# First layer of a hybrid diffusion backbone on one core: where the modulation chunks run

## What is computed

```python
for l in range(DEPTH):                                   # DEPTH = 2
    sh1, sc1, g1, sh2, sc2, g2 = split(silu(c) @ w_ada[l] + b_ada[l], 6)   # modulation, one row per stream
    hm = modulate(rmsnorm(x, norm_pre_mix[l]), sh1, sc1)
    rq, rk, rv, rg, nq, nk, nv = split(hm @ w_in[l])
    y_ret = retention_output(retention_bidir(rq, rk, rv), rg)              # 4 heads
    y_na = neighbourhood_attention(nq, nk, nv, cached keys and values)     # 8 heads of 64
    g_ret, g_na = split(sigmoid(hm @ w_gate[l]), 2)
    x = x + g1 * rmsnorm((g_ret * (y_ret @ w_ret_out[l]) + g_na * (y_na @ w_na_out[l])) @ w_o[l])
    hf = modulate(rmsnorm(x), sh2, sc2)
    x = x + g2 * rmsnorm((silu(hf @ w_ffn_gate[l]) * (hf @ w_ffn_up[l])) @ w_ffn_down[l])
```

## Time and profile before

| | us |
|---|---|
| median of 3 runs | 2136.46 |
| lowest and highest run | 2135.92, 2137.36 |
| profiled execution: span from its first to its last instruction | 2134.6 |
| median less that span (what lies around the span; the profiled execution's own time is not noted apart from it) | 1.9 |

### The profile page before, as it was taken

The page is one execution under the profiler, slowest core; times in us unless marked ns, Lnnn a source line. Parts: engine busy times, 40 slices in busy tenths (PEclk is TensorE's granted clock), DMA queues, the critical chain, the costliest instruction groups (busy, mean ns, idle before and its releaser), DMA issues.

```text
span 2134.6 us, 34256 instructions
## 1 busy us (share of the span) xinstructions
PE 2103.7 (99%) x14114; PEld 2011.7 (94%) x14114; DVE 1545.8 (72%) x2477; ACT 931.8 (44%) x1494; POOL 101.6 (5%) x195
## 2 busy tenths in 40 slices
PE   7999999999999999999999999999999999999998
PEld 6999999999989999999889999999999899999997
DVE  5688767477757887887877886755864668787786
ACT  5655432476334433332476554225753544233332
POOL 0000010110000000000000000001100000000000
PEclk9999999999999999999999999999999999999999
DMA  7333354233334222222433333532233322222223
GB/s 301 114 118 128 104 172 144 99 101 133 134 115 162 70 81 98 80 79 80 168 131 101 117 119 134 166 126 80 85 119 129 129 60 80 79 80 81 98 79 138
DMA packets 63099, 246.08 MB, mean 115 GB/s; under 512 B 7776, under 2 KB 8064, under 8 KB 60256
## 3 DMA queue, kind: packets, MB, share of 16 engines
q1 hardware_dynamic: 42336, 158.55, 21.7%
q0 software_dynamic: 20608, 85.35, 11.4%
HBM read 230.20 MB, written 13.66 MB: 114 GB/s over the span
## 4 chain that ended last, share of the span: by engine, by line
PE 91%; DVE 5%; ACT 2%; DMA 1%; issue 1%; DVEq 1%; SPq 0%; ACTq 0%
PE unit L496 11%; PE unit L497 11%; PE unit L498 11%; PE unit L508 9%; PE unit L511 9%; PE unit L509 9%; PE sc L496 4%; PE sc L497 4%; PE sc L498 4%; PE tp L496 4%; PE tp L497 4%; PE tp L498 4%; PE tp L839 1%; DVE junk L1780 1%; PE sc L815 1%
## 5 line engine op out<-in xcount | busy, mean ns | idle before, releaser
L508 PE MATMUL unit<-hmh,wh 128*128 128x320 f32 x1120 | 337.8, 309 | 1.9 <-DVE sig L2209 1.1
L509 PE MATMUL unit<-hml,wh 128*128 128x320 f32 x1120 | 337.3, 309 | 0.0
L1678 DVE TENSOR_TENSOR wl<-raw,wh 128x1024 fp32r<-128x1024 f32 x204 | 246.8, 1221 | 123.0 <-ACT wh L1184 121.0
L511 PE MATMUL unit<-hmh,wl 128*128 128x320 f32 x1120 | 255.2, 309 | 0.0
L1184 ACT ACTIVATE wh<-raw 128x1024 fp32r<-128x1024 f32 x204 | 210.1, 1050 | 95.6 <-DMA raw<-w_main 95.6
L1780 DVE CUSTOM_DVE_ANT_0 junk<-ada,csb,par 128x1024 f32<-128x1024 f32 x160 | 205.5, 1284 | 31.5 <-DMA ada<-w_ada 12.1
L508 PEld LDWEIGHTS unit<-hmh,wh 128*128 128x128 f32 x1120 | 210.2, 188 | 2.6 <-issue 2.6
L509 PEld LDWEIGHTS unit<-hml,wh 128*128 128x128 f32 x1120 | 210.3, 188 | 0.0
L496 PE MATMUL unit<-wh,hmh 128*128 128x256 f32 (+1 forms) x640 | 199.2, 311 | 1.5 <-ACT qks L1298 1.5
L497 PE MATMUL unit<-wl,hmh 128*128 128x256 f32 (+1 forms) x640 | 198.0, 309 | 0.0
L498 PE MATMUL unit<-wh,hml 128*128 128x256 f32 (+1 forms) x640 | 198.0, 309 | 0.0
(11 more groups left out here) (458 smaller groups left out, 5297.1 us busy)
## 6 DMA issues: line engine op xcount, KB each, us to landing
raw<-w_main SPq DMA_DIRECT2D x276, 512.0 KB, 4.0
ada<-w_ada POOLq DMA_DIRECT2D x80, 512.0 KB, 4.5
first<-w_first SPq DMA_DIRECT2D x8, 1024.0 KB, 19.3
x<-x_keep POOLq DMA_DIRECT2D x3, 2560.0 KB, 10.2
bias<-biases POOLq DMA_DIRECT2D x32, 192.0 KB, 2.7
x_keep<-x POOLq DMA_DIRECT2D x10, 512.0 KB, 2.9
bias<-biases POOLq DMA_DIRECT2D x16, 256.0 KB, 4.1
gains<-g_rows POOLq DMA_DIRECT2D x4, 1024.0 KB, 6.2
```

What stands on the lines that cost most here:

```text
L508: pe.matmul(u[:, h, 0:n], a[0], xs[h][0], start=f, stop=False)
L509: pe.matmul(u[:, h, 0:n], a[0], xs[h][1], start=False, stop=False)
L511: mm = pe.matmul(u[:, h, 0:n], a[1], xs[h][0], start=False, stop=z)
L1678: dve.tensor_tensor(wl[slot[i]][:, :], raw[slot[i]][:, :], f32(wh[slot[i]][:, :]), ALU.subtract)\
```

## The change

It moves chunks of the first layer to other places in VectorE's program and their loads to other places in GpSimd's; the number of chunks, and every other instruction of every engine, stays. In the gates and merges of retention, chunks go from the third and the fourth gate column of j = 0 (one each) and from behind the first two merges of j = 0 (one each). Eight come in at attention's values: four ahead of each of the two value pairs. In attention's output, one chunk behind the second and one behind the fourth merge of J = 0 go, and one more comes in at the first and one at the last gate column of J = 1. The four chunks in the channel mixer's first gated product go. GpSimd issues 13 loads for the gates instead of 17, eight behind the first biases of attention and ahead of the store of the context values (`v_out`), still eight at attention's output, and none in the channel mixer. The staging tile of that store, `nvst`, overlapped `junk` and moves to another address.

```diff
+VALUES_ADA, OUTPUT_ADA = 8, 8
@@ buffers
-        nvst = Map(n1.p - Z)("nvst", [P, NS])
+        nvst = Map(B)("nvst", [P, NS])
@@ GpSimd
-                modulation(FIRST_ADA - 12 - HEADS_ADA[0] if l == 0 else LAST_ADA - HEADS_ADA[1])
+                modulation(FIRST_ADA - VALUES_ADA - OUTPUT_ADA - HEADS_ADA[0] if l == 0 else LAST_ADA - HEADS_ADA[1])
...
                     if p == 0:
+                        if l == 0:
+                            modulation(VALUES_ADA)
                         g.wait_ge(nvst_ready, l * 2 + 2)
                         g.dma_start(v_out[l], nvst[:, :]).then_inc(nv_saved, 16)
...
-                    modulation(8)
+                    modulation(OUTPUT_ADA)
...
                 if l == 0:
-                    modulation(4)
                     g.wait_ge(ada_done, FIRST_ADA)
@@ VectorE, gates and merges of retention
                         elif j or c >= 2:
-                            modulation(((0, 0, 1, 2 - l), (2, 1, 2, 1))[j][c])
+                            modulation(((0, 0, l, 1), (2, 1, 2, 1))[j][c])
...
-                        if c < 3 or j == 0:
+                        if c < 3 and (l or j) or c > 1 and j == 0:
                             modulation(2 if l == 0 and j and c == 1 else 1)
@@ VectorE, attention's values
                 for n in range(2):
                     ps = slice(n * 2, n * 2 + 2)
+                    if l == 0:
+                        modulation(VALUES_ADA // 2)
                     wait_hi()
@@ VectorE, attention's output
-                            modulation((2, 0)[n - 2] if J == 0 else (1, 1, 1, 0)[n])
+                            modulation((2, 0)[n - 2] if J == 0 else (2, 1, 1, 1)[n])
...
-                        if l == 0 and J == 0 and c in (1, 3):
-                            modulation(1)
@@ VectorE, gate_up
-                        if l == 0 and b == 0 and n == 1:
-                            modulation(4)
```

## The result

| | before | after |
|---|---|---|
| median of 4 runs each, side by side, us | 2136.71 | 2145.55 |
| lowest and highest run, us | 2135.92, 2137.36 | 2144.88, 2145.78 |
| span of the profiled execution, us | 2134.6 | 2143.7 |

The ratio is 1.0040, with a 95% interval from 1.0028 to 1.0052. The changed kernel is slower; the forecast was 2144.0 us in a range from 2140.0 to 2148.4.

A forecast was written before the change was run, and what follows sets the result against it. TensorE, busy 99% of the span, bounds the kernel; stalls set by in-order VectorE add in full. 7.95 + 0.9 + 1.4 - 1.48 - 1.14 = 7.6 us on 2136.46, forecast 2144.0 us, range 2140.0 to 2148.4.

The forecast's parts named there:

- The reduces' 5.7 us at the third value unit: Attention's values: four chunks ahead of the `nv` subtractions exceed VectorE's 5.52 us of idle; TensorE waits 5.7 us more.
- The gates: Retention's gate merges: with chunks gone, the merge runs at 294.75 and TensorE's stall goes; gain 1.48 us.
- The mixer: Channel mixer's first gated product: without the four chunks ahead of it, TensorE's stall goes; gain 1.14 us.
- The first half of the output: Attention's output: the first chunk still waits 3.68 us for its load, so the 1.72 us stall at `mtmp` stays.
- The second half: Attention's output: the last column's extra chunk delays `mtmp` and TensorE's third product; cost 1.4 us, bounds 0 and 2.8.
- The fall of the clock at the first stall: Attention's values: not counted as a cost; only a fall behind the second stall counts, 1.7 us.
- the loads: Slab ahead of the values: lands later beside four chunk loads; cost 0.9 us, bounds 0 and 2.8.
- the 2.2 us predicted there: First attention scores: the second four chunks delay the next `nv`, so TensorE waits 2.2 us more.
- the dear rival: Attention's values: slab 1.9 us later still and clock fall of 1.7 us, 11.2 us in all, 2147.7 us; chance 0.18.

The follow-up runs named there:

- the last experiment: The changed kernel, with the first four of its eight loads for the values issued ahead of GpSimd's wait for the merges: 2143.34 us, ratio 1.0031.

## Why the prediction was right, and where it missed

The forecast was 1.6 us too low, and its reason holds: the idle time of VectorE at the values is not where the chunks were put, so they push `nv`, and TensorE with it.

**Right.** The reduces' 5.7 us at the third value unit: 5.74 without the loads. The gates: the stall is gone, 1.7 us by the starts for 1.48 predicted; the merge came at 291.06 and not at 294.75, since the subtraction that I had let keep its time runs early as well, but nothing hangs on that. The mixer: gone, 1.3 us for 1.14. In both the successor gains the difference because a stall's row counts from the modelled end of the last product. The first half of the output: 1.72 us before and after, since the chunks ahead of the first product stayed. The prediction also names the wait for the first one's load; with one chunk fewer the stall went although that wait stayed, so it is the number that counts. The second half: 1.41 us for 1.4, but half of it one step earlier, at the transposes that wait for `scales_ffn` (the `flag` row), and only half by `mtmp`. The fall of the clock at the first stall: it came (0.50 for 10.24 us) and was nearly free (0.8 us, below).

**Mis-sized: the loads.** The term was 0.9 us with an upper bound of 2.8; it measured 2.9 (8.67 less 5.74), as the slab took 7.9 us and not 5.8. In another profiled run of the same instructions (attention's output in its old order) it was 1.5, with a slab of 6.5 us. The first wait follows the slab: 4.66, 5.74, 7.27 and 8.67 us for slabs that landed after 3.9, 5.0, 6.5 and 7.9. The step that failed is the choice between two rows: I took the slab behind four chunk loads (5.8) over the slab among the bias loads (7.7). The six bias loads alone do not hold the slab up: without the chunk loads it landed in 5.0 us. The four chunk loads do, since they landed late themselves, 8.9 us after their issue in the median of the last three, and the last of them was still moving until the slab had landed. Whether they were late because GpSimd had issued the bias loads ahead of them is not shown: four such loads from 272.7 us on before, with none ahead of them, landed after 3.8 to 6.4 us, but no run took the bias loads away. The slab, which SyncE issues, landed after 7.9 us with GpSimd's four loads beside it, after 5.0 without any and after 3.9 with the four moved ahead.

**Mis-sized: the clock.** I took the loss from the 3.41 us at a granted clock of 0.50 in the earlier trace rows, half of it, 1.7 us, and found it hidden: the chunks ahead of `nv` were to run until 418.4, 15.2 us after the unit's start, and the copy was to be done after 14.7 (13.0 in the earlier trace rows and the 1.7). Half clock lasted 10.24 us. TensorE's third unit was copied 14.51 us after its start (403.76 to 418.27) and not 11.78 (397.46 to 409.24), 2.7 us later, and the 0.77 us that VectorE waits at 419.51 are what stuck out. That is also why no wait stands ahead of the scores: the 2.2 us predicted there were spent at half clock. The clock came back to 1.00 at 409.96, 6.2 us of work after the wait had ended. No run shows the 1.7 us for one fall that stands in the dear rival's sum: at the earlier trace rows none of it reached the kernel's time, the 10.24 us here cost 0.8, and the 3.41 us behind the second stall of the last experiment 1.5.

My reading of the earlier trace rows needs a correction too: the 1.7 us that I took as lost there did not lengthen the kernel. With the spread chunks the clock stays at 1.00 at that place, behind a wait of 2.23 us, and the time that TensorE has in hand goes into its next waits. TensorE's timeline there, first before (it follows the row at 1068.62 in the earlier trace rows) and then with the spread chunks:

```profile
1083.61 1.09 PE L562 MATMUL sc<-ident,xs 128*128 128x128 f32 x8 [0.46 <-ACT xs L1665]
```

```profile
1064.13 1.09 PE L563 MATMUL sc<-ident,xs 128*128 128x128 f32 x8 [2.23 <-ACT xs L1665]
...
1071.51 1.09 PE L563 MATMUL tp<-ident,xs 128*128 128x128 f32 x8 [0.81 <-ACT xs L1665]
...
1079.13 1.09 PE L563 MATMUL sc<-ident,xs 128*128 128x128 f32 x8 [1.06 <-ACT xs L1665]
```

From the first of these products to the last it takes 14.99 us with the fall and 15.00 without it.

**The sum.** 2.0 us more for the loads and 0.8 for the clock, 0.4 less at the gates and the mixer: 7.6 becomes 10.0. The profiled execution shows 9.8 for the stages that the change touches; its span is only 9.1 longer because the untouched heads ran 0.7 us shorter, which is chance, and the medians differ by 8.8. So the forecast's error, 1.6 us, is a little smaller than that of its terms, 2.4. The dear rival had both of its causes come true, the late slab and the fallen clock, but not its price: it wanted a fall behind the second stall, and there was no second stall. In the last experiment there is one, with a fall behind it that costs 1.5 us of the 1.7 that the rival gave it.

## What to carry to other kernels

Where the consumer works strictly in order, idle time belongs to a place: 26.9 us of idle time did not hold 22.2 us of work put ahead of two rows, while 11.1 us of it, one piece ahead of each row that had more than one piece's idle time in front of it, cost nothing, and that kernel is 0.24% faster than before. Moved work brings its loads along, and their price falls on whatever transfer is next on the path (here the slab ahead of the values: 7.9 us to landing with the four loads beside it, 5.0 without): look at what lands beside them in the new place, with everything that was already moving there. And a stall that a clock fall follows is read together with the next stall on the same engine: the one may eat the other (here 10.24 us at a clock of 0.50 ate the 2.2 us predicted ahead of the scores; with the clock at 1.00 a wait of 1.76 us stood there).

## What the runs showed of the hardware that I had not expected

After the one wait at the values TensorE's granted clock stood at 0.50 for 10.24 us (waits of 8.7 us in the changed kernel and of 7.3 us with the output in its old order), for 6.83 us (wait of 5.7 us, reduces without loads) and for 3.41 us (wait of 4.7 us, loads earlier); with 70 small transposes in the wait it did not fall. A wait's length alone does not settle it: near the place of the earlier trace rows all eight profiled runs have a wait of 1.9 to 2.2 us, with the clock at 0.50 for 3.41 us behind it in five of them and no fall in three (TensorE kept at work, chunks spread, loads earlier). And the 512 KB slab ahead of the values landed in 3.9 to 5.0 us in the four kernels that have no chunk loads beside it, and in 6.5 to 7.9 us in the four that have them.
